# Moving the last four condition halves out of the output products of a two-layer decoder trunk

## What is computed

```python
cond = jax.nn.silu(c)
for l in range(DEPTH):                      # DEPTH = 2
    mod = cond @ w_ada[l] + b_ada[l]        # 1024 x 6144 of weights per layer
    sh1, sc1, g1, sh2, sc2, g2 = [m[:, None, :] for m in jnp.split(mod, 6, axis=-1)]
    h = rms_norm(x, norm_mix[l]) * (1.0 + sc1) + sh1
    ...                                     # projections, GLA and windowed attention, gates
    x = x + g1 * (merged @ w_out[l])
    h2 = rms_norm(x, norm_ffn[l]) * (1.0 + sc2) + sh2
    y = moe_ffn(h2.reshape(B * S, D), w_router, b_router, w_gate[l], w_up[l], w_down[l])
    x = x + g2 * y.reshape(B, S, D)         # 16 experts, the best 2 for each token
```

## Time and profile before

| what | value |
|---|---|
| median of the runs | 1501.91 us (1497.25 to 1502.76) |
| profiled execution, its own time | 1501.6 us |
| its span from first to last instruction | 1499.9 us |
| granted TensorE clock, mean | 0.969 of full |
| PE busy | 1383.6 us, 92% of the span |
| DVE, ACT, POOL busy | 65%, 48%, 20% |

### The profile page before, as it was taken

How to read it: one execution, slowest core, us unless ns; L and a number is a source line. 1 busy time by engine, 2 the same in 40 slices (tenths; PEclk the granted TensorE clock), 3 DMA queues, 4 the chain that set the end, 5 groups by cost and what they waited for, 6 DMA issues and landing times.

```text
span 1499.9 us, 18822 instructions
## 1 busy us (share of the span) xinstructions
PE 1383.6 (92%) x7109; PEld 1093.3 (73%) x7110; DVE 982.4 (65%) x934; ACT 726.9 (48%) x776; POOL 294.9 (20%) x255
## 2 busy tenths in 40 slices
PE   3999999999999899999949999999998899999893
PEld 1776877666677788888738787788787788888572
DVE  4334575324477899999971567632657889999294
ACT  4324355122155677777652536513325677777260
POOL 1000000000015244545220000000003334544130
PEclk9999999999999999999979999999998999999997
DMA  9766302776684899999842230131355899999365
GB/s 299 270 225 233 132 1 85 259 246 218 218 330 145 301 365 393 386 378 380 316 133 85 85 113 1 57 112 57 140 213 194 296 347 366 374 377 386 147 248 192
DMA packets 157267, 341.37 MB, mean 228 GB/s; under 512 B 17150, under 2 KB 19394, under 8 KB 157186
## 3 DMA queue, kind: packets, MB, share of 16 engines
q1 hardware_dynamic: 141170, 316.97, 58.4%
q0 software_dynamic: 16016, 23.30, 4.6%
HBM read 350.68 MB, written 23.61 MB: 250 GB/s over the span
## 4 chain that ended last, share of the span: by engine, by line
PE 77%; DVE 7%; DMA 6%; ACT 3%; issue 3%; DVEq 2%; SPq 1%; POOL 0%; POOLq 0%; ACTq 0%
PE PS L1180 15%; PE PS L1181 14%; PE PS L1182 14%; PE PS L1576 7%; PE PS L1580 7%; PE PS L1584 7%; PE PS L1114 3%; PE PS L1564 2%; DMA ring<-in_w_ada 2%; DMA ring<-in_w_down 1%; ACT reg L934 1%; DVE ring_parts L2190 1%; DMA y_rows<-reg,icur 1%; PE PS L1589 1%; SPq L475 1%
## 5 line engine op out<-in xcount | busy, mean ns | idle before, releaser
L1180 PE MATMUL PS<-ring_parts 128*128 128x512 f32 (+1 forms) x704 | 276.7, 393 | 9.5 <-DVE hT_parts L1820 5.9
L2190 DVE TENSOR_TENSOR ring_parts<-ring,reg_parts 128x2048 fp32r<-128x2048 f32 x124 | 278.1, 2284 | 3.4 <-ACT reg_parts L1038 3.4
L1038 ACT ACTIVATE reg_parts<-ring 128x2048 fp32r<-128x2048 f32 x124 | 230.6, 1909 | 67.4 <-DMA ring<-in_w_down 35.3
L1812 DVE TENSOR_TENSOR ring_parts<-ring,ring_parts 128x2048 fp32r<-128x2048 f32 (+1 forms) x52 | 112.9, 2210 | 153.9 <-ACT ring_parts L856 153.9
L1180 PEld LDWEIGHTS PS<-ring_parts 128*128 128x128 f32 x704 | 133.3, 189 | 63.9 <-issue 31.0
L856 ACT ACTIVATE ring_parts<-ring 128x2048 fp32r<-128x2048 f32 (+1 forms) x52 | 93.4, 1845 | 151.9 <-DMA ring<-in_w_in 113.4
L2190 DVE TENSOR_TENSOR ring_parts<-ring,hT_parts 128x2048 fp32r<-128x2048 f32 x68 | 155.2, 2287 | 13.5 <-issue 13.0
L1182 PE MATMUL PS<-ring_parts 128*128 128x512 f32 x384 | 150.5, 392 | 0.0
L1181 PE MATMUL PS<-hT_parts,ring_parts 128*128 128x512 f32 x384 | 150.5, 392 | 0.0
L1038 ACT ACTIVATE hT_parts<-ring 128x2048 fp32r<-128x2048 f32 x68 | 126.5, 1909 | 14.0 <-DMA ring<-in_w_gate 8.0
L1584 PE MATMUL PS<-ring_parts,reg_parts 128*128 128x512 f32 x528 | 130.6, 389 | 0.0
(11 more groups left out here) (328 smaller groups left out, 2406.2 us busy)
## 6 DMA issues: line engine op xcount, KB each, us to landing
ring<-in_w_up SPq DMA_DIRECT2D x32, 2048.0 KB
ring<-in_w_gate SPq DMA_DIRECT2D x32, 2048.0 KB, 12.5
ring<-in_w_down SPq DMA_DIRECT2D x32, 2048.0 KB
ring<-in_w_ada SPq DMA_DIRECT2D x40, 1024.0 KB, 5.3
ring<-in_w_in SPq DMA_DIRECT2D x16, 2048.0 KB
ring<-in_w_ada SPq DMA_DIRECT2D x4, 2048.0 KB, 12.4
ring<-in_w_out SPq DMA_DIRECT2D x4, 2048.0 KB
reg<-y_rows SPq DMA_DIRECT2D x16, 512.0 KB, 6.3
```

Of the source, the lines that this page charges most:

```text
L1038: act.activation(high[:, cols], ring[:, 3 * k + part, cols], ACT.Copy).then_inc(w_hi[part], 1)
L1180: pe.matmul(out_, left[0], right[0], start=first, stop=False)
L1812: tt(ring_r[:, unit_slot(n), cols], w, ring_r[:, 2 + n % 2, cols].bitcast(F32), ALU.subtract).then_inc(lo_done, 1)
L2190: tt(ring_r[:, 3 * k + part, cols], ring[:, 3 * k + part, cols], high[:, cols].bitcast(F32), ALU.subtract).then_inc(w_lo[part], 1)
```

## The change

The four halves 36 to 39 (`next_half(20)` to `next_half(23)`) leave the output products' stage. Two of them stand behind the gate rows, before the ranks, in place of 8 of the 16 spare products, and two stand in place of 9 of the 18 spare products before the first expert's tokens. The condition columns go from between product 6 and the transposes of the tokens 1 to the place between the first expert's gate and up products, and DVE's copy of the bank goes from behind product 4 to behind the low parts of the first expert's gate weights. SP loads the halves 38 and 39 behind the fifth of the experts' weights instead of ahead of all of them, and the down weights of expert 1 after everything else, when all halves are used. In layer 1 nothing changes.

```diff
-    MIX_HALVES = (4, 4, 4, 4, 4, 4, 0)
+    MIX_HALVES = (4, 4, 4, 4, 4, 0, 0)
...
-                load_halves(visits(W_O0))
-                if l < DEPTH - 1:
-                    sp.wait_ge(ada_used, halves_used(l + 1))
                 sp.wait_ge(out_ready, at(out_ready, l, NT))
                 load_expert(l, 0, 0, 1)
                 load_expert(l, 1, 1, 0)
-                load_expert(l, 1, 1, 2)
+                if l == DEPTH - 1:
+                    load_expert(l, 1, 1, 2)
                 sp.wait_ge(out_ready, at(out_ready, l, 2 * NT))
-                for e, part in ((0, 0), (0, 2), (1, 1)):
-                    load_expert(l, e, e, part)
+                load_expert(l, 0, 0, 0)
+                load_expert(l, 0, 0, 2)
+                if l < DEPTH - 1:
+                    for number in range(first_half(l + 2) - 2, first_half(l + 2)):
+                        load_ada_half(number)
+                load_expert(l, 1, 1, 1)
+                if l < DEPTH - 1:
+                    sp.wait_ge(ada_used, halves_used(l + 1))
+                    load_expert(l, 1, 1, 2)
...
-                    if i < 4:
-                        next_half(20 + i)
-                    elif i == 4:
+                    if i == 4:
...
-                        if l < DEPTH - 1:
-                            condition_columns(MIX_ADA_BANK, l + 4)
                         router_tokens(1)
...
-                spare_products(16, 4)
+                next_half(20)
+                next_half(21)
+                spare_products(16 if l == DEPTH - 1 else 8, 4)
...
-                spare_products(18, 4)
+                spare_products(18 if l == DEPTH - 1 else 9, 4)
+                next_half(22)
+                next_half(23)
                 transposed_tokens(0, 0, 0)
                 spare_products(4, 4)
                 gate_product(0, 0)
+                if l < DEPTH - 1:
+                    condition_columns(MIX_ADA_BANK, l + 4)
...
-                        if l < DEPTH - 1:
-                            condition_rows(MIX_ADA_BANK, halves_used(l + 1))
...
                 weights_low(0, 0, 0)
+                if l < DEPTH - 1:
+                    condition_rows(MIX_ADA_BANK, halves_used(l + 1))
```

## The result

| kernel | median of its runs | profiled execution (span, mean granted clock) |
|---|---|---|
| before | 1501.25 us (1494.38 to 1504.16, 11 runs) | 1501.6 us (1499.9, 0.969) |
| changed | 1491.32 us (1487.23 to 1498.53, 11 runs) | 1495.14 us (1493.5, 0.969) |

The ratio is 0.9938 (95% interval 0.9922 to 0.9954), that is 9.3 us faster, and 6.9 to 11.7. The two profiled executions differ by 6.5 us.

The account below looks back on a forecast made before the run. The prediction took PE, with 77% of the chain, as the bound, and DVE's small instructions in the router's stretch. Its terms, -7.2 + 0.35 + 0 + 0.9 + 0.3 = -5.65 us, gave 1496.0 us, range 1491.5 to 1500.5.

Parts of the forecast that it names:

- The stage: Layer 0's output products: removing four halves, the columns and PE's 1.4 us wait for half 37 saves 7.2 us.
- The halves before the ranks: Router's stretch: two halves added to PE and 8 of 16 spare products removed cost 0.35 us, ends 0 and +0.6.
- The slack of 0.26: Before DVE's read of the ranks in layer 0, PE's spare products have only 0.26 us to spare.
- The halves before the transposes: Before the first expert's tokens, two halves replacing nine spare products fit into PE's wait for the gather: cost 0.
- The columns: Condition columns between the first expert's gate and up products, where PE is the bound, cost 0.9 us.
- The gather: Fetch of the first expert's tokens, now beside expert 1's up weights at its start only, costs 0.3 us.
- The row of the loop (6.5): Gathers in the experts' loop, beside the weights' stream, take 6.5 us in the median from issue to landing.
- More than the sum: Rival, chance 0.16: layer 1's 1.20 us wait, the ranks' and gather's costs fall away, 1494; columns too, 1493.
- The gather's rival: Rival, chance 0.20: late loads make the first tokens' gather cost 1.4 to 3.4 us, total 1497 to 1499.
- The clock's: Rival, chance 0.10: PE's clock rises late around layer 0's gate rows, at worst +1.2 us, 1497.2.
- The slower one: Rival, chance 0.04: half 39 lands late, delaying the first expert; gain gone if it lands at 463.4 us.

Follow-up runs that it names:

- the early half 37: The kernel before with half 37 loaded ahead of the second output weights instead of behind them; 1496.7 us, ratio 0.9975.
- the last experiment: The changed kernel with expert 1's up weights loaded ahead of halves 38 and 39, which also wait for half 37's use; one execution, 1491.31 us.
- the kernel with fewer spares: The kernel before with 8 and 9 spare products in place of 16 and 18, nothing moved; 1502.08 us, ratio 1.0009.
- the padded one: The changed kernel with 62 additions of zero to a register at PE's start; 1496.94 us, ratio 0.996.
- both: The changed kernel with condition columns before the first transposes and expert 1's last two loads held until the gathered tokens are there; 1495.27 us, ratio 0.9959.

## Why the prediction was right, and where it was not

The forecast was 1496.0 us with a range of 1491.5 to 1500.5. The mechanism came as described up to the first transposes. The gain was larger: 6.6 and 9.3 us by two measurements and 7.7 at equal clock, against 5.65.

*The stage* (-7.2). 54.0 - 46.9 = -7.1. Each part is borne out: the halves and the wait by the kernel without them, the wait also by the early half 37 (in its waits; its time has an interval of 1.2 to 6.3 us), the pitch of 5.45 as in layer 1.

*The halves before the ranks* (+0.35). Measured 0. The slack of 0.26 was right (0.2), but the term was mis-sized: it took the 1.23 us by which a half spreads two large products, or its bare length of 1.0. Side by side two halves take 1.88, 0.94 each, exactly what eight spare products give back. With the clock down it is another matter: +1.5 in the last experiment.

*The halves before the transposes* (0). Measured 0, with 1.8 to 2.1 us of wait left. Half 39 had more cover than PE needed, and with 2 MB put ahead of it its wait of 0.92 us still ended before the gather did.

*The columns* (+0.9). Measured 0.94 by their removal from that place.

*The gather* (+0.3). Measured +0.2 to +0.7 between any profile of before and of the changed kernel, +0.5 in the mean of all. The size came near by luck, since its reason was wrong. It was put at the overlap with "the first of its five us only", but the prediction's own numbers have the loads flow until 456.8 and the gather run from 453.8 (458.96 - 5.14), which are three us, and a little more than three were measured. It stayed cheap because the first three do not count: the data of a gather move in its fourth us. The row of the loop (6.5) would have made it 1.4. The Trainium skill (DMA: Bandwidth & Descriptors, section "Queues, rings and completion order") says that a DMA engine takes turns between the queues that have work for it, packet by packet, and gives no size. The trace agrees with it in direction, since the gather became slower beside the loads, and not with the prediction's reading, that the gather pays for as long as a load flows.

*What was missing.* These terms give -7.1 + 0 + 0 + 0.94 + 0.5 = -5.7 us, the forecast's sum. That the sums agree so closely is partly luck: 0.35 too much before the ranks stands against 0.2 too little for the gather and 0.1 in the stage. Up to x0 the marks bear the sum out (82.25 and 81.97 us from the issue before, 75.59 and 75.29 changed: 6.7, and 5.7 with the columns behind it). But from x0 to x5 the changed kernel takes 85.33 and 85.88 us, before 87.37 and 87.55. With the 0.94 of the columns taken out it gained 2.4 to 3.2 us there, and of it 1.7 to 2.3 are PE's waits "issue", which shrank from 5.2 to 2.9 and 3.5. No term had them. That they shrink without any half being moved is shown by the kernel with fewer spares. That the length of the code ahead is the cause is supported by it and by the padded one, which brought back only part. It is not the only one: "both" has the short code and 5.17 us, with loads beside them. So at x5 the changed kernel is 8.5 us ahead, counted from the issue (160.9 and 161.2 against 169.6 and 169.5). At the last down product of the layer it is 7.0 to 8.4 (366.3 and 364.9 against 373.3 and 373.0), and 7.7 by the times at equal clock. The 1.6 from there to the 9.3 of the first measurement are not placed. The mean clock of its executions was 0.9716, that of the second measurement 0.9695, and that of the kernel before over its 92 executions 0.9700. By the slope, 0.0016 are 1.4 us.

*The rivals.* "More than the sum" had the size (1494, 1493) and two of its reasons. The ranks' term fell away. And layer 1's wait of 1.20 us for the ranks went, though not in the first profile. This is DVE's read of them in layer 1, in the changed kernel and in its second profile.

```profile
1130.18 0.23 DVE L2166 TENSOR_TENSOR reg<-PS,reg 128x64 f32<-128x64 f32 x1 [1.17 <-PE PS L1557]
```

```profile
1127.69 0.23 DVE L2166 TENSOR_TENSOR reg<-PS,reg 128x64 f32<-128x64 f32 x1
```

Behind product 7 of layer 1 these are 16.24 and 15.15 us. All five profiles of the old order have the wait (16.08 to 16.32). Of the nine of the new order seven have none (15.14 to 15.16), and only the changed kernel's first and the padded one have it. In the five us that begin some 11 us behind product 7 the clock was 0.81 in the first profile and 0.97 in the second. The old order without the halves reached layer 1 as early as the changed kernel and kept the wait, so coming earlier is not enough, and why it goes is open. It is worth 1.1 us, which no term of the sum has, to most executions profiled in the new order. The seven profiles without it have mean clocks of 0.971 to 0.978, those with it 0.965 to 0.970, so a time at equal clock takes part of it away. Of the rival's other reasons, the gather's term did not fall away.

The rival's chance was 0.16, and that of a gain above 0.5% was 0.20. The first measurement is beyond 0.5% (0.62%), the second is not (0.44%). The gather's rival did not come. The clock's came in two of the nine profiles that have a stage without halves and could show it (1.1 us in the old order without them, 1.5 in the last experiment). The slower one was tried and its cover held.

## What to carry to other kernels

Price an instruction group by what stands beside it in its new place: the same half cost 1.23 us between large products and 0.94 in a row of small ones. A layer that has the stage without the moved work gives the best price of its removal, here within 0.1 us. Before an edit's gain is explained, profile both kernels twice and compare between marks, and when the number of instructions or the loads beside them change, read the waits that have no releaser: they can give or take 2 us in code that nobody touched. Look for them where the code is passed for the first time. Before a transfer's overlap is priced, look in a window of each us when it moves its data: the gather paid only for loads in its fourth.

## What the runs showed that I had not expected

PE waits up to 2.9 us at a few places of the experts' code with no releaser in the profile. The places change with what stands ahead: in front of the transposes for expert 3 before and with 9 spares fewer, one transpose before their end when padded, two matmuls behind them with 17 fewer. One place, before the sixth transpose for expert 1 in the kernels with the changed kernel's code length, has a wait of 1.54 or 2.87 us with loads beside it and none without. All of them stand in the first pass through the code, and the six later passes of the loop have none. By what rule they move within it is open.

The time of one and the same kernel goes with its mean granted clock, 0.88 us for each 0.001, and its executions spread over some 10 us (1490.21 to 1500.68 in the second measurement of the changed kernel). Which of the two sets the other is not shown.
